# Reordering ScalarE and VectorE inside the seven-product pairs of a feed-forward layer, and the hand-over to its output product

## The reference, cut to what matters

```python
def swiglu(x, w_in, w_out):
    a, b = jnp.split(x @ w_in, 2, axis=-1)
    return (jax.nn.silu(a) * b) @ w_out
...
h = h + FFN_RES * swiglu(rmsnorm(h, g_ff1[i]), w_ff1_in[i], w_ff1_out[i])
```

## Time and profile before

| what | value |
|---|---|
| median of 3 runs | 3236.87 us (3235.92 to 3239.73) |
| the profiled execution | 3238.2 us, span 3236.3 us |
| PE busy | 3049.0 us, 94% of the span |
| DVE busy | 2138.7 us, 66% |
| ACT busy | 1424.2 us, 44% |

### The profile page before, as it was taken

How to read it: one execution, slowest core, us unless ns; L and a number is a source line. 1 busy time by engine, 2 the same in 40 slices (tenths; PEclk the granted TensorE clock), 3 DMA queues, 4 the chain that set the end, 5 groups by cost and what they waited for, 6 DMA issues and landing times.

```text
span 3236.3 us, 52020 instructions
## 1 busy us (share of the span) xinstructions
PE 3049.0 (94%) x19012; PEld 2585.8 (80%) x19012; DVE 2138.7 (66%) x3013; ACT 1424.2 (44%) x2295; POOL 623.3 (19%) x480
## 2 busy tenths in 40 slices
PE   7999999999899999999989999899999999999998
PEld 4888887877699887667789887799887667799886
DVE  5665665364688746776698744888438776788645
ACT  3655555452455423334455522555323334455422
POOL 0303212183611110000211112111110000311112
PEclk9999999999999999999999999999999999999999
DMA  6112022123222222211222322223222112222222
GB/s 239 55 43 58 16 57 58 38 76 121 74 103 91 88 101 74 69 66 65 98 91 91 106 90 89 85 91 104 82 87 85 66 59 78 92 103 91 95 96 75
DMA packets 94911, 270.91 MB, mean 84 GB/s; under 512 B 35440, under 2 KB 36592, under 8 KB 93424
## 3 DMA queue, kind: packets, MB, share of 16 engines
q1 hardware_dynamic: 94016, 267.89, 24.8%
q0 software_dynamic: 320, 1.05, 0.1%
q10 hardware_dynamic: 432, 0.02, 0.0%
HBM read 263.68 MB, written 5.24 MB: 83 GB/s over the span
## 4 chain that ended last, share of the span: by engine, by line
PE 60%; DVE 16%; issue 10%; ACT 7%; POOL 2%; DMA 1%; SPq 1%; DVEq 1%; ACTq 1%; POOLq 0%
PE bank L149 14%; PE bank L150 13%; PE bank L151 13%; DVE raw_pair L2271 4%; ACT block_hi L2136 2%; PE bank L2019 2%; PE bank L2021 2%; PE bank L2020 2%; DVE block_lo L2296 2%; DVE differences L2270 2%; PE bank L2454 1%; ACT weights_hi L137 1%; PE bank L1598 1%; PE bank L2475 1%; DVE weights_lo L142 1%
## 5 line engine op out<-in xcount | busy, mean ns | idle before, releaser
L142 DVE TENSOR_TENSOR weights_lo<-weights_raw,weights_hi 128x1024 fp32r<-128x1024 f32 (+2 forms) x258 | 393.2, 1524 | 378.2 <-ACT weights_hi L137 376.2
L137 ACT ACTIVATE weights_hi<-weights_raw 128x1024 fp32r<-128x1024 f32 (+2 forms) x258 | 296.2, 1148 | 471.8 <-PE bank L151 453.8
L149 PE MATMUL bank<-x_hi,weights_hi 128*128 128x512 f32 x832 | 336.4, 404 | 13.7 <-DVE weights_lo L2219 7.1
L2019 PE MATMUL bank<-sum_hi,block_hi 128*128 128x256 f32 x960 | 280.2, 292 | 63.1 <-ACT bank L2155 60.6
L150 PE MATMUL bank<-x_lo,weights_hi 128*128 128x512 f32 x832 | 327.2, 393 | 0.0
L151 PE MATMUL bank<-x_hi,weights_lo 128*128 128x512 f32 x832 | 327.1, 393 | 0.0
L2390 POOL TENSOR_TENSOR t<-t,t 128x512 f32<-128x512 f32 x88 | 144.6, 1643 | 869.3 <-ACT t L2104 869.3
L149 PE MATMUL bank<-hidden_hi,weights_hi 128*128 128x512 f32 x704 | 275.5, 391 | 9.5 <-DVE t L2254 9.5
L150 PE MATMUL bank<-hidden_lo,weights_hi 128*128 128x512 f32 x704 | 275.3, 391 | 0.0
L151 PE MATMUL bank<-hidden_hi,weights_lo 128*128 128x512 f32 x704 | 275.1, 391 | 0.0
L2020 PE MATMUL bank<-sum_lo,block_hi 128*128 128x256 f32 x960 | 271.8, 283 | 0.0
(11 more groups left out here) (452 smaller groups left out, 7838.7 us busy)
## 6 DMA issues: line engine op xcount, KB each, us to landing
raw_pair<-w_ff1in SPq DMA_DIRECT2D x42, 1024.0 KB, 4.9
raw_pair<-w_ff2in SPq DMA_DIRECT2D x42, 1024.0 KB, 4.9
weights_raw<-w_mix SPq DMA_DIRECT2D x72, 512.0 KB, 3.2
weights_raw<-w_ff1out SPq DMA_DIRECT2D x32, 704.0 KB, 4.1
weights_raw<-w_ff2out SPq DMA_DIRECT2D x32, 704.0 KB, 4.0
weights_raw<-w_tail SPq DMA_DIRECT2D x42, 512.0 KB, 3.3
mod_weights<-w_mod SPq DMA_DIRECT2D x6, 2048.0 KB, 16.4
weights_raw<-w_dn SPq DMA_DIRECT2D x24, 512.0 KB, 3.6
```

Source lines behind the costliest of these rows:

```text
L137: nc.scalar.activation(K.wh[:, slot, 0:cols], K.raw[:, slot, 0:cols], ACT.Copy).then_inc(S.wh_ready, 1)
L142: nc.vector.tensor_tensor(K.wl[:, slot, 0:cols], K.raw[:, slot, 0:cols], K.wh[:, slot, 0:cols].bitcast(F32), ALU.subtract).then_inc(S.raw_ ...
L149: nc.tensor.matmul(out, K.wh[:, slot, a:b], xh, start=start, stop=False)
L2019: nc.tensor.matmul(out, hi[:, a], x[0][:, k, :], start=start and k == 0, stop=False, skip_group_check=True)
```

## The change

Four things are moved.

1. On ACT, within a pair, `silu` of the pair before comes ahead of `seed_a`, and `first_hi` of the next pair comes after the first `seed_b` and `hidden_hi` instead of ahead of both.
2. On DVE, the first two differences of the next pair come ahead of `fourth_lo`; the third (`second`) and the last (`fourth`) follow it directly; `first_lo` comes after `hidden_lo`.
3. In the last pair of a stage PE computes FOURTH ahead of the `b_left` product, and DVE does `scale_a` ahead of `sum_b`.
4. Also in the last pair, ACT makes the high part of the first output slab between `hidden_hi` and the second `seed_b`, and `silu` of the last pair comes ahead of the high part of the second slab.

```diff
@@ ff_pe, half_pair
             product(half_out(p, "a_right"), *block(THIRD), sums(3)).then_inc(S.product_done, 1)
-            product(half_out(p, "b_left"), K.bxh[:, 1, :], K.bxl[:, 1, :], sums(4)).then_inc(S.slab_done, 1)
+            if not end:
+                product(half_out(p, "b_left"), K.bxh[:, 1, :], K.bxl[:, 1, :], sums(4)).then_inc(S.slab_done, 1)
             pe.wait_ge(S.seeded, left("seeded") + 4 * n + 4)
             pe.wait_ge(S.diff_ready, left("diff_ready") + 2 * n + 2)
             product(half_out(p, "a_right"), *block(FOURTH), half_x("22")).then_inc(S.slab_done, 1)
+            if end:
+                product(half_out(p, "b_left"), K.bxh[:, 1, :], K.bxl[:, 1, :], sums(4)).then_inc(S.slab_done, 1)
@@ ff_act, half_pair
             fourth_hi(j)
+            silu(j - 1, start)
             seed_a(j, p)
-            silu(j - 1, start)
             keep_fifth(j)
-            if not end:
-                first_hi(j + 1, 1 - p)
             seed_b(j, p, "b_left", 3)
             hidden_hi(j - 1)
+            if end:
+                act.wait_ge(S.raw_full[0], 8 * s0 + 16 * (FT // 2) + 16)
+                nc.scalar.activation(K.wh[:, 0, 0:1408], K.raw[:, 0, 0:1408], ACT.Copy).then_inc(S.wh_ready, 1)
+            else:
+                first_hi(j + 1, 1 - p)
             seed_b(j, p, "b_right", 5)
@@ ff_act, after the last pair
+        silu(FT - 1, True)
+        act.wait_ge(S.raw_full[1], 8 * s0 + 16 * (FT // 2) + 32)
+        act.wait_ge(S.slab_done, s1 + 1)
+        nc.scalar.activation(K.wh[:, 1, 0:1408], K.raw[:, 1, 0:1408], ACT.Copy).then_inc(S.wh_ready, 1)
...
-        split_hi(act, s1, 0, 1408)
-        split_hi(act, s1 + 1, 1, 1408)
-        silu(FT - 1)
         hidden_hi(FT - 1)
@@ ff_dve, half_pair
             plain_block_lo(j, p)
+            if not end:
+                differences(j + 1, 1 - p)
             fourth_lo(j)
             if not end:
-                differences(j + 1, 1 - p)
-                first_lo(j + 1, 1 - p)
+                second(j + 1, 1 - p)
+                fourth(j + 1, 1 - p)
             hidden_lo(j - 1)
             if not end:
-                fourth(j + 1, 1 - p)
+                first_lo(j + 1, 1 - p)
                 second_lo(j + 1)
+                sum_b(j, p)
+                scale_a(j, p)
             else:
                 split_lo(dve, s1, 0, 1408)
-            sum_b(j, p)
-            scale_a(j, p)
+                scale_a(j, p, True)
+                sum_b(j, p, True)
```

More of the change, by code:

```diff
@@ L2022, in product, with half_pair @@
             return last
-        def half_pair(j, p, first=False):
+        def half_pair(j, p, first=False, end=False):
             n = HALF_PAIRS * f + j - PLAIN_PAIRS
@@ L2055, in ff_pe @@
                 half_pair(2 * i + PLAIN_PAIRS + 2 - p, p)
-        half_pair(FT - 1, 1)
+        half_pair(FT - 1, 1, end=True)
         s1, v1 = K.slab(l, ("ff1out", "ff2out")[w]), K.evic(l, ("ff1out", "ff2out")[w])
@@ L2248, in scale_plain, with sum_b @@
             nc.vector.tensor_copy(K.t2[:, :], pb[3 * j + 1][:, :]).then_inc(S.evac, 1)
-        def sum_b(j, p):
-            dve.wait_ge(S.slab_done, s0 + 2 * j + 1 + CREDIT)
+        def sum_b(j, p, end=False):
+            dve.wait_ge(S.slab_done, s0 + 2 * j + (2 if end else 1) + CREDIT)
             dve.wait_ge(S.seeded, left("seeded") + 4 * number(j) + 4)
@@ L2254, in sum_b, with scale_a @@
             nc.vector.tensor_tensor(two(K.t2[:, :]), half_rows(p, "b"), wide(K.s5[:, :], 1, 2), ALU.add).then_inc(S.evac, 1)
-        def scale_a(j, p):
-            dve.wait_ge(S.slab_done, s0 + 2 * j + 2 + CREDIT)
+        def scale_a(j, p, end=False):
+            dve.wait_ge(S.slab_done, s0 + 2 * j + (1 if end else 2) + CREDIT)
             nc.vector.tensor_tensor(two(K.t1[:, :]), half_rows(p, "a"), two(rstd[:, :]), ALU.mult).then_inc(S.evac, 1)
@@ L2266, in differences @@
             n = number(j)
-            w11, w21, w12, w22 = (raw_pair[p][:, 512 * i:512 * i + 512] for i in range(4))
+            w11, _, w12, w22 = (raw_pair[p][:, 512 * i:512 * i + 512] for i in range(4))
             dve.wait_ge(S.raw_full[p], 8 * s0 + 16 + 8 * (j + p))
@@ L2271, in differences, with second @@
             nc.vector.tensor_tensor(w12, w12, w11, ALU.subtract).then_inc(S.diff_made, 1)
-            dve.wait_ge(S.diff_made, left("diff_made") + 4 * n + 2)
-            nc.vector.tensor_tensor(K.df[:, 0, :], w22, w12, ALU.subtract).then_inc(S.diff_made, 1)
+        def second(j, p):
+            dve.wait_ge(S.diff_made, left("diff_made") + 4 * number(j) + 2)
+            nc.vector.tensor_tensor(K.df[:, 0, :], raw_pair[p][:, 1536:2048], raw_pair[p][:, 1024:1536], ALU.subtract)\
+                .then_inc(S.diff_made, 1)
         def fourth(j, p):
@@ L2321, in ff_dve @@
         differences(PLAIN_PAIRS, 0)
+        second(PLAIN_PAIRS, 0)
         fourth(PLAIN_PAIRS, 0)
```

## The result

The changed kernel takes 3149.79 us (median of 4 runs, 3144.8 to 3150.93), the kernel before 3236.39 us beside it. The ratio is 0.9727, 95% interval 0.9711 to 0.9744: 2.7% faster, 87 us, within 83 to 94. The forecast was 3149. Two later groups of runs of the changed kernel gave 3147.3 and 3151.3 (ratios 0.9724 and 0.9745), so the size of the gain is known to some 3 us.

A forecast was written before the change was run, and what follows sets the result against it. PE bounds the kernel, stalled mainly by THIRD's wait for seed_b. Gains of 74.2 + 3.5 + 7.1 + 3.2 = 88.0 us from 3238.2 give 3150.2, less 1.3 for the median 3148.9, said as 3149; range 3138 to 3170.

The forecast's parts named there:

- What bounds: PE, busy 94%; its largest wait, THIRD for ACT's seed_b copy, 76 times, costs 1.03 us a pair.
- `seed_b` ahead of `first_hi`: On ACT in pairs 3 to 20 of each stage: THIRD's stall goes, 72 x 1.03 = 74.2 us.
- The three chains: ACT's queue, DVE's load and weight loading could be late next; spare 0.5, 0.55 and about 5 us.
- (a): ACT: silu now ahead of seed_a, done 2.3 to 2.4 us into the pair; SECOND wants it at 2.88; spare 0.5 us.
- (b): DVE's own load: 9.45 us a pair, fitting in 10.0 with 0.55 us to spare.
- (c): Weights: a pair's 1 MB lands 4.9 us after issue, about 5 us to spare before the first difference.
- The first pair: First seven-product pair of each stage: gain between 0.5 and 1.6 us a stage, middle 0.9, 3.5 us in all.
- The hand-over: Last pair to output product: 2.5 us gap goes, FOURTH's new wait costs 0.7; net 7.1 us, bounds 0 and 10.
- Clock behind it: After the hand-over in f = 1 and f = 3 PE's clock should no longer fall to 0.50: 3.2 us, bounds 0 and 3.2.
- The total: Gains sum to 88.0 us, giving 3149 us; the summed forecast's own band, 3138 to 3153, had 0.74.
- POOL kept waiting: Rival: POOL's product waits in each pair until the gap behind the third difference; costs 0 to 14 us, about 3156; 0.11.
- Slower, by the ring over `silu`: Rival: silu waits for DVE's scale_a, holding up SECOND's copy, if DVE's load exceeds 11.05 us a pair; 3255; 0.03.

The follow-up runs named there:

- the kernel with the other hand-over: Changed kernel with the last pair's products in the old order and the first output tile waiting for one evacuation fewer: 3147.01 and 3144.50 us in two groups.
- the last three experiments: Old last-pair product order, one evacuation fewer: 3147.01, 3144.50 us; on that, first pair's hidden_hi and hidden_lo later: 3139.66; instead, DVE waiting for POOL in first pair: 3148.14.

## Why the prediction was right, point by point

- **What bounds.** Right. The 76 waits went, and the stall was worth the distance between starts (1.03 us), not the idle column (0.79). By the column the 72 pairs would have given 57 us; they gave 74.0.
- **`seed_b` ahead of `first_hi`.** The term 74.2 was measured as 74.0, and each time in it came out within about 0.1 us. What I had not seen when I wrote it is that DVE's new order would do the same alone; I had that order down as costing nothing.
- **The three chains.** (a) `seed_a` done at T+2.30 (2.3 to 2.4 forecast). (b) Slack 0.48 (0.55 forecast), and the kernels with more work on DVE measured it: 0.3 us more cost nothing, 1.2 us more made the pair 10.61. (c) No wait for the raw weights appeared among PE's.
- **The first pair.** 5.0 for 3.5, within its bounds of 2 to 6.4 in sum but not by my reasons: two of the four stages lie outside the 0.5 to 1.6 that I gave for one, so here the number was luck in part. In f = 0 the gain was 3.7 us: PE's standing still ahead of the plain product was cut from one distance of 2.35 us to 1.85 (1.14 ahead of SECOND instead of 0.61), and the clock, at 0.50 for 6.8 us behind it before, stays at 1.00. In f = 1 and f = 3 it was only 0.5, since POOL's product took 6.2 us and FOURTH had a new wait of 1.1 us behind it. In f = 2 it was 0.3. PE in f = 0, before and then after:

```profile
888.69 0.38 PE L2019 MATMUL bank<-x_hi,plain_block_hi 128*128 128x256 f32 x1 [2.07 <-DVE plain_block_lo L2286]
...
878.46 0.38 PE L2019 MATMUL bank<-x_hi,plain_block_hi 128*128 128x256 f32 x1 [1.58 <-DVE plain_block_lo L2296]
```

- **The hand-over.** Net 7.5 for 7.1, with FOURTH's 0.74 us as worked out.
- **Clock behind it.** Right at the place: it stays at 1.00, so the 1.2 GHz stretches of 3.0 and 3.4 us are gone, and the output products are 3.6 us shorter. In the sum the 3.2 us are not found. In the five profiled executions with the old hand-over the output products take 481.9 us in the mean and the stretches between and behind them 974.0; in the nine with a new one it is 477.9 and 977.8. Together that is 1455.9 and 1455.7 us. By these means what is won behind the hand-over is lost again further on; in the two executions of the table the clock is at 0.50 for longer there. Whether the one causes the other stays open.
- **The total.** That 3149 was met within 1 us is partly luck. The first pairs and the hand-over gave 1.9 us more than forecast, the clock nothing in sum, and groups of runs of the same kernel differ by up to 4 us. Two small sums in the prediction are also off: the hand-over's 1.8 x 4 is 7.2, not 7.1, and 3149 less three times 3 is 3140, not 3138; neither changes a reading.
- **POOL kept waiting.** As a rival for every pair, wrong: in the loop of the changed kernel it got in at once. But its mechanism is what happened in the first pair of f = 1 and f = 3, where the product lasted until the gap behind the third difference, which I had named as the next one. The rule of the Trainium skill, "SBUF — State Buffer", section "Who interferes with whom", that whoever issues first holds the pair for its whole instruction, is written there for DVE's two-port modes; for two SBUF inputs the section says that they contend. Taken for these operations too, it agrees with the DVE operations that stood for POOL; for POOL it does not, by the 6.23 and 3.99 us rows. The measurements decide.
- **Slower, by the ring over `silu`.** Not in this kernel; the wait appears with 1.2 us more on DVE, so its condition was rightly stated.

**What POOL's two outcomes cost in the first pair.** The two profiled executions of the kernel with the other hand-over show it in f = 3, where the same code did either. In one the product took 6.26 us, and PE reached the plain product after a distance of 1.03 us. In the other it took 1.97 us, lengthened the `sum_lo` operation ahead of `plain_block_lo`, and PE stood for 3.08. POOL and PE, the first execution and then the second:

```profile
2747.74 6.26 POOL L2405 TENSOR_TENSOR t<-t,t 128x512 f32<-128x512 f32 x1 [9.66 <-ACT t L2107]
...
2750.49 0.39 PE L2019 MATMUL bank<-x_hi,plain_block_hi 128*128 128x256 f32 x1 [0.75 <-DVE plain_block_lo L2296]
...
2744.52 1.97 POOL L2405 TENSOR_TENSOR t<-t,t 128x512 f32<-128x512 f32 x1 [8.12 <-ACT t L2107]
...
2749.90 0.39 PE L2019 MATMUL bank<-x_hi,plain_block_hi 128*128 128x256 f32 x1 [2.80 <-DVE plain_block_lo L2296]
```

The first intervals were 11.35 and 12.84 us. But PE had also reached the pair at different times: in the first execution its clock was at 0.50 for 3.4 us of the plain pair ahead, in the second at 1.00. Counted from one operation of DVE near the start of the stage (the reciprocal that makes `rstd`, at 2728.86 and 2727.17) to the second `fourth_hi`, both took 28.9 and 28.7 us. So by these two executions the row of DVE's operations sets the time of a first pair, and the length of POOL's product by itself says little about it. The same pattern with 3.08 us, and the clock at 0.50 for 3.4 us behind it, makes the 14.3 us of f = 2.

What stays open: why POOL gets in at once in some pairs and is kept waiting in others with the same operations side by side. The product's starts that I looked at fall inside a DVE operation in both kinds; I found no distance that tells them apart.

## What to carry to other kernels

Where a short copy frees the busiest engine, it should not stand behind a long operation that waits for a third engine; and such a stall may have two conditions, either of which is enough to lift, as here, so try each alone before you keep both. Read the price of a stall from the starts of the instructions, not from the idle column, when the records overlap. Before you reorder, add up the next engine's load for a period and find where its slack shows as a wait: here 0.48 us in 10, and a test that adds more than that (1.2 us here) tells you what becomes the bound.

## What the runs showed of the hardware that I had not expected

- A POOL product of 128x512 that reads two tiles of the same memory as DVE lengthened one DVE operation by 1.0 to 1.1 us, whichever it fell on, for 84 of the 88 products of the changed kernel's stages (0.68 to 1.78 and 1.22 to 2.31 us); the other four lengthened none. With DVE's operations back to back it may itself wait for 5 us (6.23 us where others take 1.29), and a gap of 0.12 us, where a DVE operation waits for the result of the one ahead of it, lets it in.
- The part of the kernel up to the first `fourth_hi`, the same in all of them, took 873.5 to 883.8 us in the profiled executions, with the granted clock of its first eight stretches of 100 us between 0.97 and 1.00. The two shortest had the clock at 0.50 for 23.9 us of it, the longest for 37.5. That scatter of 10 us is larger than the effect of the last three experiments.
